# Decoder trunk with expert routing: the index look-up of the routing on one 512-wide buffer, three operations where there were six

## The reference, cut to what matters

```python
def peer(h, wq, subkeys, u_tab, v_tab):
    q = (xt @ wq).reshape(t, PEER_HEADS, 2, PEER_HALF)
    sc = jnp.einsum('thpc,pkc->thpk', q, subkeys, preferred_element_type=jnp.float32)
    sv, si = lax.top_k(sc, PEER_TOPK)                                   # 16 best of 128 keys, twice
    cand = sv[:, :, 0, :, None] + sv[:, :, 1, None, :]                  # 16 x 16 sums
    cidx = si[:, :, 0, :, None] * PEER_NKEYS + si[:, :, 1, None, :]
    cs, cpos = lax.top_k(cand.reshape(t, PEER_HEADS, -1), PEER_TOPK)    # 16 best of 256 sums
    idx = jnp.take_along_axis(cidx.reshape(t, PEER_HEADS, -1), cpos, axis=-1)
    gate = jax.nn.softmax(cs, axis=-1)
    ...
        act = jax.nn.gelu(jnp.einsum('td,tkd->tk', xbb, u_tab[ib], ...))
        return jnp.einsum('tk,tkd->td', gb * act, v_tab[ib].astype(jnp.float32))
```

## Time and profile before

| what | us |
|---|---|
| median of 3 runs | 1639.1 |
| lowest and highest of them | 1638.93, 1649.3 |
| the profiled execution | 1638.64 |
| its span, first to last instruction | 1636.5 |
| PE busy | 1365.2 |
| DVE busy | 1141.5 |
| ACT busy | 759.3 |
| POOL busy | 588.8 |
| moved by the transfers | 607.22 MB, mean 371 GB/s |

### The profile page before, as it was taken

The page is one execution under the profiler, slowest core; times in us unless marked ns, Lnnn a source line. Parts: engine busy times, 40 slices in busy tenths (PEclk is TensorE's granted clock), DMA queues, the critical chain, the costliest instruction groups (busy, mean ns, idle before and its releaser), DMA issues. The chain is left out here.

```text
span 1636.5 us, 15247 instructions
## 1 busy us (share of the span) xinstructions
PE 1365.2 (83%) x3816; PEld 623.7 (38%) x3816; DVE 1141.5 (70%) x2821; ACT 759.3 (46%) x2074; POOL 588.8 (36%) x517
## 2 busy tenths in 40 slices
PE   7999789888597888787989788887898988777776
PEld 3544334333242343443444344444434432222222
DVE  2337865657656989998565799898865476666764
ACT  2324542544334756654353655656433354444443
POOL 0025233344233343353332344344333254443441
PEclk9999899999799899998999998999799999999999
DMA  9569999989699999899999998989899899999996
GB/s 359 189 244 388 395 380 391 405 354 417 266 413 417 390 361 347 346 375 364 354 415 411 416 415 331 347 336 375 308 399 416 320 416 421 422 421 422 421 421 254
DMA packets 106406, 607.22 MB, mean 371 GB/s; under 512 B 9296, under 2 KB 9424, under 8 KB 40784
## 3 DMA queue, kind: packets, MB, share of 16 engines
q0 software_dynamic: 73728, 536.90, 81.6%
q1 hardware_dynamic: 32592, 69.37, 11.5%
HBM read 605.19 MB, written 1.05 MB: 370 GB/s over the span
## 5 line engine op out<-in xcount | busy, mean ns | idle before, releaser
L869 PE MATMUL ps<-rings,dgs 128*128 128x512 f32 x2048 | 1006.3, 632 | 217.3 <-ACT dgs L626 216.8
L434 POOL DMA_INDIRECT rings<-in_uv_tab_dram,idx x512 | 587.5, 1147 | 981.5 <-PE ps L869 886.7
L1264 DVE CUSTOM_DVE_ANT_0 rings<-rings,h 128x1024 f32<-128x1024 f32 x512 | 614.0, 1223 | 163.5 <-DMA rings<-in_uv_tab_dram,idx 146.7
L869 PEld LDWEIGHTS ps<-rings,dgs 128*128 128x128 f32 x2048 | 387.5, 199 | 768.8 <-ACT dgs L626 385.9
L620 ACT ACTIVATE gel<-dots 128x1 f32<-128x1 f32 x512 | 102.8, 201 | 567.3 <-DVE dots L1264 557.5
L626 ACT ACTIVATE dgs<-cst,wgt 128x128 f32<-128x128 f32 x512 | 205.5, 401 | 37.2 <-issue 2.5
L676 PE MATMUL ps<-wst,hT 128*128 128x512 f32 x384 | 179.2, 605 | 9.7 <-DMA wst<-in_wq_dram 7.3
L623 ACT ACTIVATE wgt<-gel,share 128x1 f32<-128x1 f32 x512 | 150.8, 295 | 37.4 <-issue 2.8
L676 PEld LDWEIGHTS ps<-wst,hT 128*128 128x128 f32 x384 | 73.8, 195 | 102.7 <-issue 101.2
L1041 DVE COPY mem<-ps 128x512 f32<-128x512 f32 x16 | 11.1, 691 | 108.3 <-PE ps L668 108.3
L620 ACT ACT_TABLE_LOAD x56 | 71.8, 1283 | 1.7
(11 more groups left out here) (173 smaller groups left out, 893.6 us busy)
## 6 DMA issues: line engine op xcount, KB each, us to landing
wst<-in_wq_dram SPq DMA_DIRECT2D x15, 2048.0 KB, 19.4
wst<-in_w_out_dram SPq DMA_DIRECT2D x4, 2048.0 KB, 19.7
rings<-in_uv_tab_dram,idx POOLq DMA_INDIRECT x512, 10.5
wst<-in_glu_w_dram SPq DMA_DIRECT2D x4, 2048.0 KB, 26.7
rings<-in_w_in_dram SPq DMA_DIRECT2D x3, 2048.0 KB, 16.6
vec<-in_vecs_dram SPq DMA_DIRECT2D x11, 512.0 KB, 11.4
rings<-in_w_in_dram SPq DMA_DIRECT2D x2, 1024.0 KB, 8.7
dgs<-in_w_in_dram SPq DMA_DIRECT2D x1, 2048.0 KB, 19.4
```

The lines of the kernel that those rows point to most:

```text
L434: nc.gpsimd.indirect_dma_start(out=ring[:, g % RING, :], out_offset=None, in_=uv_tab, in_offset=bass.IndirectOffsetOnAxis(ap=idx[n % 4][:, ...
L869: ins = PE.matmul(ps[:, 4 + 2 * t + b, :], diag[:, g % DIAGS, :], ring[:, g % RING, D + b * BANK:D + (b + 1) * BANK], start=(g % (PH * TOP ...
L1264: V.tensor_tensor_reduce(out=u, in0=u, in1=h[:, t, :], scale=1.0, scalar=0.0, op0=ALU.mult, op1=ALU.add, accum_out=dots[n % 2][:, s:s + 1] ...
```

## The change

`cand_a` and `cand_b` become the two halves of one buffer `cand` of 512 elements a partition. In `route_index` the three pairs of instructions over 256 elements become three instructions over 512. `hot` views `cand` as 32 rows of 16, and `hot2` views it as 2 x 16 x 16, for which `top_f` is repeated along the middle axis. The drains stay as they are. All other uses of the two buffers keep their shapes.

```diff
@@ buffers
-        cand_a, cand_b = sb("cand_a", [P, 256]), sb("cand_b", [P, 256])
-        key_b = cand_b[:, :].rearrange("p (a k) -> p a k", a=2)
+        cand = sb("cand", [P, 512])
+        cand_a, cand_b = cand[:, 0:256], cand[:, 256:512]
+        key_b = cand_b.rearrange("p (a k) -> p a k", a=2)
@@ ahead of the routing
-            hot = [c[:, :].rearrange("p (a b) -> p a b", a=TOPK) for c in (cand_a, cand_b)]
+            hot = cand[:, :].rearrange("p (a k) -> p a k", k=TOPK)
+            hot2 = cand[:, :].rearrange("p (i a k) -> p i a k", i=2, k=TOPK)
@@ route_index
                 dve.drain()
-                for p in range(2):
-                    V.tensor_tensor(hot[p], bc(pos_ab[:, p, :], [None, TOPK]), bc(iota16, [TOPK, None]), ALU.is_equal)
-                dve.drain()
-                for p in range(2):
-                    V.tensor_tensor(hot[p], hot[p], bc(top_f[:, p, :], [TOPK, None]), ALU.mult)
-                dve.drain()
-                for p in range(2):
-                    V.tensor_reduce(row[:, p, :], hot[p], AX.X, ALU.add)
+                V.tensor_tensor(hot, bc(pos_ab[:, :, :].rearrange("p i a -> p (i a)"), [None, TOPK]),
+                                bc(iota16, [2 * TOPK, None]), ALU.is_equal)
+                dve.drain()
+                V.tensor_tensor(hot2, hot2, top_f[:, :, :].unsqueeze(2).to_broadcast([P, 2, TOPK, TOPK]), ALU.mult)
+                dve.drain()
+                V.tensor_reduce(row[:, :, :].rearrange("p i a -> p (i a)"), hot, AX.X, ALU.add)
                 dve.drain()
```

More of the change, by code:

```diff
@@ L1213, in route_pairs @@
                     V.max_index(top_i[:, p, 8:16], top[:, p, 8:16], key_b[:, p, :])
-                V.tensor_tensor(cand_a[:, :].rearrange("p (a b) -> p a b", a=TOPK), bc(top[:, 0, :], [None, TOPK]),
+                V.tensor_tensor(cand_a.rearrange("p (a b) -> p a b", a=TOPK), bc(top[:, 0, :], [None, TOPK]),
                                 bc(top[:, 1, :], [TOPK, None]), ALU.add)
@@ L1220, in route_best @@
                 top_cs = cs[n % 2]
-                V.max(top_cs[:, 0:8], cand_a[:, :])
+                V.max(top_cs[:, 0:8], cand_a)
                 V.tensor_scalar(top_f[:, 0, :], top_i[:, 0, :], float(NK * (n // (T * PH))), None, ALU.add)
@@ L1224, in route_best @@
                 dve.drain()
-                V.max_index(pos_i[:, 0:8], top_cs[:, 0:8], cand_a[:, :])
-                V.match_replace(cand_b[:, :], top_cs[:, 0:8], cand_a[:, :], LOWEST)
+                V.max_index(pos_i[:, 0:8], top_cs[:, 0:8], cand_a)
+                V.match_replace(cand_b, top_cs[:, 0:8], cand_a, LOWEST)
                 V.tensor_scalar(ncs[n % 2][:, :], top_cs[:, 0:1], -1.0, None, ALU.mult)
                 dve.drain()
-                V.max(top_cs[:, 8:16], cand_b[:, :])
+                V.max(top_cs[:, 8:16], cand_b)
                 dve.drain()
-                V.max_index(pos_i[:, 8:16], top_cs[:, 8:16], cand_b[:, :]).then_inc(cs_ok, 1)
+                V.max_index(pos_i[:, 8:16], top_cs[:, 8:16], cand_b).then_inc(cs_ok, 1)
                 dve.drain()
```

## The result

The changed kernel takes 1632.74 us (median of 12 runs, 1623.69 to 1636.2), the kernel before 1639.01 us (12 runs, 1630.3 to 1649.3). The ratio is 0.9948, with a 95% interval from 0.9923 to 0.9972. The forecast was 1636.9 us. The time lies in the range that was given, but the gain, 6.3 us by the medians and 8.5 us (4.6 to 12.6) by the ratio, is about three to four times the 2.2 us that were forecast, and the first question is what it is made of. The ratio is not simply the quotient of the two medians.

The account below looks back on a forecast made before the run. DVE was taken to set the pace in the two S5 stretches, transfers or other waits elsewhere. Twelve S5 routings at 0.20 us, times 0.93 and 0.90, gave 1.1 + 1.1 = 2.2 us: 1639.1 to 1636.9 us, range 1631 to 1642.

Parts of the forecast that it names:

- One routing: In each routing's look-up, three instructions over 512 take 2.29 us where three pairs took 2.49, saving 0.20 us.
- durations add up: Rival: each removed instruction is worth its duration, so a routing saves 0.45 us, giving 1634.2 or 1624.7 us; chance 0.04.
- The S5 stretches: From 514 to 790 and 928 to 1222 us DVE sets the pace; six routings in each save 1.1 us.
- The other 20: Routings outside the S5 stretches, where fetches, weight loads or PE are awaited, count for nothing.
- cover: Outside the S5 stretches the ring's 8 buffers hold work ahead, hiding the saving; without it 19 routings bring 3.8 us.
- The sum: Whole kernel: 1.1 + 1.1 = 2.2 us less, from a median of 1639.1 to 1636.9 us.
- the last stretch: Sign: the expert steps from 1344 us to the end, set by the fetches, stay as long as before.
- Hidden altogether: Rival: the saving is spent in DVE's waits in the S5 stretches too, leaving 1639.1 us within 1 us; chance 0.22.
- All 32 count: Rival: no cover exists and every routing's 0.20 us counts, 6.4 us, giving 1632.7 us; chance 0.05.
- A weight load collides: Rival: after an S5 stretch, earlier fetches delay a weight load and PE waits 5.2 us more, giving 1642.1; chance 0.12.
- The multiply at half rate: Rival: three dimensions slow the look-up's multiply, losing 0.33 us a routing, 3.6 us on 12, giving 1642.7; chance 0.02.

Follow-up runs that it names:

- the doses: Kernel before with memsets added in 12 or 20 routings (ratios 1.0041, 1.0017), or look-up left out in 4, 12 or 20 (0.9924, 0.9874, 0.9964).
- the 20 alone: Kernel before with three wide instructions only in the 20 routings outside the S5 stretches: ratios 0.9994 and 1.0, together 0.9997.

## Why the prediction was right and where it was wrong

*One routing.* Right: 2.29 us for 2.49, from starts and not from durations. The rival that durations add up would have needed 2.07 us and falls with the timeline. The prediction took its 0.45 us from the Trainium skill's page VectorE: DVE Perf Modes, section "The DRAIN you can't avoid". That section goes on to say that a next operation that is not held starts earlier, which the prediction left out. The start after 0.34 us behind an instruction of 0.43 us fits the section read whole, and the timeline gives 0.20 us.

*The S5 stretches.* The mechanism was right: DVE sets the pace. The term of 2.2 us for 12 routings, at 0.93 and 0.90, measured 2.47 us over ten of them by the marks, so 3.0 us over 12, which takes in whatever the gaps brought; by the doses, with 0.83 to 1.15 for each microsecond, 2.0 to 2.8 us; by the fit, at 0.95, 2.3 us. The sizing took the share of time in which DVE does not wait as the share of the saving that counts. The size comes out close, but the reason does not hold: the wait at `s5_rot` kept its 10.2 us and moved along with DVE, so it took no share of the saving. The sum also had no term for the short gaps: 1.6 us of them from mark 17 to 22 went away with the change, an estimated 1.0 us by the fit.

*The other 20.* This is the step that failed. "The other 20 routings count for nothing" rested on cover, read from DMA shares near 1. Leaving out 49.8 us there gave 5.9 us, and adding 10.8 us cost 2.8 us, the latter not clear of zero. By these 4.0 us of saving are worth 0.5 to 1.0 us; measured directly, the 20 alone gave 0.5 us less, with an interval from 3.0 us less to 2.0 us more. And they reach into the S5 stretches as well: with only these 20 wide the step from 17 to 22 is about 1.4 us shorter, as the gaps in it are. The marks outside the S5 stretches say less. 0 to 4 is shorter by 0.57 us, with sets that overlap in one profile only, and 4 to 8 by 1.79 us, where the narrow ones alone reach over 5.5 us. From 31 to the end all six wide profiles are longer, by 0.83 us in the mean, but the step before it is shorter; from 25 to the end it is 306.06 us narrow and 306.35 us wide, so the last stretch is as long as before, as the prediction had it. The two profiles with wide instructions in the 12 alone, narrow from mark 25 on, have 66.89 and 66.94 us from 31 to the end, so it is not the width of the last routings that makes this longer.

*The sum.* S5 at 2.0 to 3.0 us and the others at 0.5 to 1.0 us give 2.5 to 4.0 us; with the fit, 2.3 us for S5, 1.0 for the gaps and 0.5 to 1.0 for the others, an estimate of 3.8 to 4.3 us. Four measurements together give 4.9 us (3.3 to 6.5), where 2.2 was forecast. So the sum was too small by about half, by a term set to nothing and one that it did not have. The first measurement of 8.5 us by its ratio was the largest gain of four; what it has above the others is scatter. That its median still lay inside the range owes more to the width of the range than to the sum. Whether a further microsecond hides in steps 0 to 8 stays open; 12 runs of a kernel with this scatter do not settle it.

*The rivals.* Hidden altogether: fallen, the S5 steps are shorter, and the wait at `s5_rot` took up nothing. All 32 count (6.4 us): the combined time does not exclude it, its interval ends at 6.5; the runs with the look-up left out or time added in the 20 do, with 0.12 and 0.26 for each microsecond. A weight load collides: the loads do scatter by several us between executions, but in both kernels and in both directions, so not as a consequence of the change. In the steps from 22 to 25 the narrow profiles alone reach from 150.24 to 157.81 us. The multiply at half rate: 694 ns, fallen.

## What to carry to other kernels

Price a merged instruction by starts, not by durations: two neighbours with no drain between them already overlap, so merging them saves the short gap (here 0.07 us of a 0.42 us instruction) and not the whole fixed part of its duration. Multiply that by the routings or loops in which the engine sets the pace, and give the covered ones a small worth rather than none. Compare two programs by marks that both have, over several profiles: one pair of traces showed a 5 us jump at a weight load that a second profile of the same program showed as well. And look at the idle time without a releaser too: where a change alters the number of instructions, such gaps can come and go in stretches that the change does not touch.

## What was not expected of the hardware

A weight load of 2 MB beside the fetches on the chain took 27.39 us in one execution of the kernel before and 24.24 us in another; over twelve profiles the load that the chain passes through in this place, starting between 1237 and 1261 us, took 23.34 to 27.39 us. The steps from mark 22 to 25, which hold such loads, differ by 5.0 us between those two executions of one program, and by up to 7.6 us between programs with the same instructions in them. The steps from mark 17 to 22 lie within 0.13 us in the four profiles without any wide routing (242.61, 242.61, 242.70 and 242.74), but 1.4 us lower in two programs whose instructions differ only elsewhere (241.24 and 241.28).

DVE has, besides those at `s5_rot`, short gaps of 0.2 to 0.5 us without a releaser in the profile, at places that are the same in every profile of a program and others in another program: 7 in the kernel before, 11 in the changed one, 2.9 and 3.7 us together.

And a memset over 256 elements cost 0.27 us from start to start, less than the 0.34 us of a tensor operation over 256, so both doses were smaller than sized.
